# Third branch of a hybrid mixer on one Trainium2 core: keys normed and the decay's input prepared between the projected tiles

## The chip, the cores and the metric

The kernel runs on one core of a Trainium2 chip. The metric is the device time of one execution in microseconds (us), as a median of several runs; lower is better. All data is f32. Five engines work side by side, each in the order of its own program, and wait for one another on semaphores: TensorE (PE; its weight loads are shown apart, as PEld), VectorE (DVE), ScalarE (ACT), GpSimd (POOL), and SyncE (SP), whose queue issues nearly all transfers.

## The reference, cut to what matters

Two layers (`DEPTH = 2`) over 256 context tokens and 256 image tokens with a model width of 1024. Each layer has a mixer of three branches (latent attention, an mLSTM, an RWKV-7 style recurrence), then 64 routed experts. The change is in the third branch, before its recurrence:

```python
r, k, v, wl, al, gl = jnp.split(centred_shift(z, mu), RW_SPLIT_IDX, axis=-1)
kk = (k * k_k).reshape(B, T, RW_HEADS, RW_N)
kk = kk / jnp.maximum(jnp.linalg.norm(kk, axis=-1, keepdims=True), 1e-12)
...
w = -jax.nn.softplus(-(w0[d] + jnp.tanh(wl_d) @ w2[d])) - 0.5
decay = jnp.exp(-jnp.exp(w))
a = jax.nn.sigmoid(a0[d] + al_d @ a2[d])
kd = k * (1 + (a - 1) * k_a)
...
g = jax.nn.sigmoid(gl) @ g2        # used once, at the branch's output
```

`z` is the layer's input times 1152 columns of `w_in`. Both directions d = 0 and 1 use the same `kk`; d = 1 runs over the tokens in reverse.

## The kernel before

Everything is held with features on the 128 partitions and the 512 tokens along the free axis. The third branch's projection makes nine tiles of 128 features, j = 0 to 8: r is in tiles 0 and 1, k in 2 and 3, v in 4 and 5, the decay's small input in 6, the rate's small input in 7, the output gate's input in 8. In the second layer tiles 0, 1 and 8 cover 256 tokens only. Each engine's part is a function, and each layer runs them in the order attention, mLSTM, third branch, merging of the branches, routing, experts.

- `rw_pe` (TensorE): tile j is 8 matmuls over the width (`project`, L292; a f32 matmul leaves two records) into bank j % 4. From j = 4 on it waits until ScalarE has copied out tile j - 4 (`zev`). After the nine tiles come, in this order: two 128x512 matmuls with a block-diagonal matrix of ones that sum the squared keys by head into banks 4 and 5 (L968; they wait for the square, `kc` 2), four small products of direction 0 with `w2` and `a2` (L986; they wait for `tl` 2) into banks 0 to 3, 32 small matmuls that turn v to rows (L992), the first of the late modulation rows (L309), then the turning of beta and kappa (L1003, waits for `prep`) and the score products (L1014).
- `rw_act` (ScalarE): copies tile j into one of two padded buffers `ZP` (L1125). After all nine: Tanh of tile 6 (L1127), Sigmoid of tile 8 (L1129), square of the keys (L1131), Ln and Exp that give the inverse norm (L1133, L1134), then for direction 0 the two sigmoids of each pair of heads (L1139, L1141), copies of the turned v (L1145), three exponentials for each pair (L1148 to L1150), and a copy of the modulation row (L315).
- `rw_dve` (VectorE): three operations shift tile j between neighbouring tokens and mix it into `Zs` (L1193 to L1195, counted in `sh`). After all nine: keys times `k_k` (L1198), the maximum with 1e-24 (L1205), keys times inverse norm (L1210). Then for each direction the prefix sum of the decay's logarithm (L1216) and its difference (L1218) for both pairs, and beta, kappa and AR (L1221 to L1234), the last of which releases L1003.

No planner orders the work: the order is the program text and the waits. SyncE's queue loads 2 MB chunks of weights into four ring slots. In this branch it loads the chunks for the late modulation rows into slots 0 and 1, each when the slot's earlier user has been read. The expert weights are issued only after the branches of that layer are merged.

Of the kernel before, what the change touches and what calls it, by code (L numbers as in the profile page):

```python
# [7 lines left out]
ALU = mybir.AluOpType  # L8
ACT = mybir.ActivationFunctionType
# [4 lines left out]
P = 128  # L14
# [143 lines left out]
def build(nc, xin, consts, smalls, wsm, wst, wexp, out):  # L158
    es = ExitStack()
    with es:  # L160
# [14 lines left out]
        WS = sb("small_weights", [P, WS_N])  # L175
# [7 lines left out]
        ps = [es.enter_context(nc.psum_tensor(f"bank{i}", [P, 512], F32)) for i in range(8)]  # L183
# [15 lines left out]
        def sm(name, j=0, n=1):  # L199
            return S_[:, SM[name] + j:SM[name] + j + n]  # L200
# [748 lines left out]
        def each_head():  # L949
            return (slice(0, 64), slice(64, 128))  # L950

        def opposite(h):

            return slice(64 - h.start, 128 - h.start)

        def rw_pe(pe, l):
            for j in range(9):
# [6 lines left out]
                if j == 1:  # L964
                    ml_turn_back(pe, l)
            pe.wait_ge(rw["kc"], l * RW["kc"] + 2)
            for i in range(2):
                last = nc.tensor.matmul(ps[4 + i][:, :], bd, YA[:, i, :], start=True, stop=True)  # L968
            last.then_inc(rw["kc"], 1)
            pe.wait_ge(rw["tl"], l * RW["tl"] + 2)  # L970
            for d in range(2):
# [10 lines left out]
                if d:  # L982
                    pe.wait_ge(rw["yc"], l * RW["yc"] + 2)
                for pr in PAIRS:
                    for i, (o, z, rows_of) in enumerate(((WS_W2, 6, hd_), (WS_A2, 7, opposite(hd_)))):
                        nc.tensor.matmul(ps[2 * pr + i][:, :], WS[rows_of, o + pr * P:o + (pr + 1) * P], Zs[rows_of, z, :], start=True, stop=True).then_inc(rw["lr"], 1)  # L986
                if d == 0:
# [117 lines left out]
            for pr in range(2):  # L1105
                last = nc.tensor.matmul(ps[2 + pr][:, c0:], bd, YA[:, pr, c0:], start=True, stop=True)
                last.then_inc(rw["ym"], 1)
            for pr in range(2):
                nc.tensor.matmul(ps[6 + pr][:, c0:], WS[:, WS_G2 + pr * P:WS_G2 + (pr + 1) * P], Zs[:, 8, c0:], start=True, stop=True).then_inc(rw["g"], 1)
# [6 lines left out]
        def rw_act(act, ch, l):  # L1116
            for j in range(9):
# [7 lines left out]
                nc.scalar.activation(dst, seg(ps[j % 4][:, :])[:, half:, :], ACT.Copy).then_inc(rw["zev"], 1)  # L1125
            act.wait_ge(rw["sh"], l * RW["sh"] + 9)
            nc.scalar.activation(Zs[:, 6, :], Zs[:, 6, :], ACT.Tanh).then_inc(rw["tl"], 1)  # L1127
            c0 = queries_from(l)
            nc.scalar.activation(Zs[:, 8, c0:], Zs[:, 8, c0:], ACT.Sigmoid).then_inc(rw["tl"], 1)  # L1129
            act.wait_ge(rw["kc"], l * RW["kc"] + 1)  # L1130
            nc.scalar.activation(YA[:, :, :], KK[:, :, :], ACT.Square).then_inc(rw["kc"], 1)  # L1131
            act.wait_ge(rw["kc"], l * RW["kc"] + 4)
            ch.link(nc.scalar.activation(KDS[:, :, :], KDS[:, :, :], ACT.Ln))  # L1133
            nc.scalar.activation(KDS[:, :, :], KDS[:, :, :], ACT.Exp, scale=-0.5).then_inc(rw["kc"], 1)  # L1134
            for d in range(2):
                mods = late_mod(l, d)
                for pr in PAIRS:
                    act.wait_ge(rw["lr"], l * RW["lr"] + 4 * d + 2 * pr + 1)
                    nc.scalar.activation(sgm[pr], ps[2 * pr][:, :], ACT.Sigmoid, bias=sm("w0", 2 * d + pr)).then_inc(rw["sg"], 1)  # L1139
                    act.wait_ge(rw["lr"], l * RW["lr"] + 4 * d + 2 * pr + 2)  # L1140
                    nc.scalar.activation(aa[pr], ps[2 * pr + 1][:, :], ACT.Sigmoid, bias=sm("a0", 2 * d + pr)).then_inc(rw["sg"], 1)  # L1141
                if d == 0:
                    for pr in PAIRS:
                        act.wait_ge(rw["tok"], l * RW["tok"] + pr + 1)
                        nc.scalar.activation(VT[pr][:, :, :], ps[4 + pr][:, :].rearrange("p (c f) -> p c f", c=NC), ACT.Copy).then_inc(rw["tokc"], 1)  # L1145
# [33 lines left out]
        def rw_dve(dve, ch, l):  # L1179
# [6 lines left out]
            for j in range(9):  # L1186
# [8 lines left out]
                nc.vector.scalar_tensor_tensor(seg(Zs[:, j, :])[:, half:, :], z[:, :, 1:257], omu[:, j:j + 1], t, ALU.mult, ALU.add).then_inc(rw["sh"], 1)  # L1195
            dve.wait_ge(rw["sh"], l * RW["sh"] + 9)
            for pr in range(2):
                last = nc.vector.tensor_scalar(KK[:, pr, :], Zs[:, 2 + pr, :], sm("k_k", pr), None, ALU.mult)  # L1198
                if pr == 0:
                    ch.add(last)  # L1200
            last.then_inc(rw["kc"], 1)

            dve.wait_ge(rw["kc"], l * RW["kc"] + 3)
            for pr in range(2):
                last = nc.vector.tensor_scalar(KDS[:, pr, :], ps[4 + pr][:, :], 1e-24, None, ALU.max)  # L1205
                if pr == 0:
                    ch.add(last)
            last.then_inc(rw["kc"], 1)
            dve.wait_ge(rw["kc"], l * RW["kc"] + 5)
            nc.vector.tensor_tensor(KK[:, :, :], KK[:, :, :], KDS[:, :, :], ALU.mult).then_inc(rw["kc"], 1)  # L1210
            dve.wait_ge(rw["kc"], l * RW["kc"] + 6)
# [1608 lines left out]
```

## Time and profile before

| | |
|---|---|
| median of 3 runs | 2665.92 us (2663.73 to 2675.43) |
| the profiled execution, its own time | 2670.35 us |
| its span in the trace | 2668.2 us, 41238 instructions |
| busy: PE, DVE, ACT, POOL | 2411.8, 785.9, 573.4, 145.9 us |
| mean granted TensorE clock | 0.949 of full |

The profile was taken of one execution, 4.43 us above the median. A row of the chain of work gives a start, a length and the instruction that the end of the kernel depended on at that time. A row of the timeline gives a start, a length, engine, line, operation, written and read tiles, and in brackets how long the engine had been idle and what ended that. The views by stretch give busy time and the granted clock, where 1.00 is the full 2.4 GHz and 0.50 is 1.2 GHz. "issue" is idle time for which the trace shows no wait.

### The profile page before, as it was taken

What the parts mean: (1) busy time and instruction counts of PE and PEld (TensorE: products, weight loads), DVE (VectorE), ACT (ScalarE), POOL (GpSimd) and SP (SyncE); (2) the same over time, 40 slices, a digit from 0 to 9 for tenths busy, and PEclk for the clock granted to TensorE, in tenths of its full rate; (3) what the DMA queues carried; (4) which work ended last, traced back from release to release, by engine and by line L of the source; (5) the groups of instructions that cost most, each with busy time, mean ns of one, the idle gap of its engine ahead of it and who ended that gap; (6) DMA issues with size and microseconds to landing.
All of it is one profiled execution on the core that took longest, in us unless ns stands there. A gap on an engine that the chain in (4) does not pass through costs nothing.

```text
span 2668.2 us, 41238 instructions
## 1 busy us (share of the span) xinstructions
PE 2411.8 (90%) x17286; PEld 1365.4 (51%) x17286; DVE 785.9 (29%) x1929; ACT 573.4 (21%) x1134; POOL 145.9 (5%) x154
## 2 busy tenths in 40 slices
PE   7999978999998898999998789978999798977997
PEld 3466467744445443333333556747788644433444
DVE  1354355311113531111111525455411521111112
ACT  3445123120003011111111144333220211100111
POOL 0000000000000011111111000000000011100100
PEclk9999989999997899999999999989999799988999
DMA  7201032521101699999999631113241599999993
GB/s 318 79 2 39 32 128 99 185 98 64 63 0 63 250 424 423 409 407 424 404 407 393 257 144 72 64 37 124 101 186 63 201 374 422 420 408 417 413 423 153
DMA packets 67640, 599.72 MB, mean 225 GB/s; under 512 B 13182, under 2 KB 13310, under 8 KB 25600
## 3 DMA queue, kind: packets, MB, share of 16 engines
q1 hardware_dynamic: 50032, 555.09, 51.3%
q0 software_dynamic: 17424, 41.99, 4.1%
q8 instruction: 137, 2.24, 0.3%
q14 instruction: 47, 0.39, 0.0%
HBM read 588.63 MB, written 26.75 MB: 231 GB/s over the span
## 4 chain that ended last, share of the span: by engine, by line
PE 79%; DMA 9%; DVE 6%; issue 4%; ACT 2%; SPq 0%; ACTq 0%; DVEq 0%
PE bank L1855 10%; PE bank L1330 9%; PE bank L292 6%; PE bank L2281 5%; PE bank L1870 5%; DMA ring<-in_wexp 3%; PE bank L1345 3%; PE bank L2295 3%; PE bank L1335 3%; DMA arena<-in_wexp 3%; PE bank L384 3%; PE bank L2301 2%; PE bank L1026 2%; PE bank L1041 2%; PE bank L309 1%
## 5 line engine op out<-in xcount | busy, mean ns | idle before, releaser
L1855 PE MATMUL bank<-ring,arena 128*32 128x512 f32 (+2 forms) x1248 | 299.1, 610 | 16.7 <-issue 14.7
L1330 PE MATMUL bank<-normed,ring 128*128 128x512 f32 (+1 forms) x768 | 255.5, 486 | 0.0
L2281 PE MATMUL bank<-ring,arena 128*32 128x512 f32 (+2 forms) x832 | 192.8, 624 | 16.5 <-issue 15.0
L1330 PEld LDWEIGHTS bank<-normed,ring 128*128 128x128 f32 x768 | 145.9, 190 | 101.8 <-issue 91.8
L1855 PEld LDWEIGHTS bank<-ring,arena 128*32 128x32 f32 (+2 forms) x1248 | 95.2, 131 | 152.6 <-issue 150.4
L292 PE MATMUL bank<-normed,ring 128*128 128x512 f32 (+1 forms) x416 | 160.2, 544 | 0.0
L1855 PE MATMUL bank<-branches,arena 128*32 128x512 f32 (+2 forms) x400 | 137.3, 610 | 8.1 <-issue 8.1
L292 PEld LDWEIGHTS bank<-normed,ring 128*128 128x128 f32 x416 | 78.4, 190 | 77.8 <-issue 75.3
L1870 PE MATMUL bank<-arena 128*32 128x512 f32 (+2 forms) x384 | 112.7, 596 | 3.9 <-DMA arena<-in_wexp 2.0
L2045 DVE TENSOR_TENSOR arena<-bank,arena 128x256 f32<-128x256 f32 x43 | 18.2, 424 | 327.5 <-ACT arena L1964 327.5
L2281 PEld LDWEIGHTS bank<-ring,arena 128*32 128x32 f32 (+2 forms) x832 | 56.1, 123 | 102.1 <-issue 102.0
L1784 POOL DMA_INDIRECT arena<-hidden_rows,block_slots x42 | 42.7, 1016 | 1186.2 <-DVE block_slots L1601 900.5
L2295 PE MATMUL bank<-arena 128*32 128x512 f32 (+1 forms) x400 | 87.2, 654 | 21.6 <-issue 21.0
L1870 PE MATMUL bank<-ring,arena 128*32 128x512 f32 (+2 forms) x440 | 102.0, 596 | 4.0 <-issue 2.0
L2281 PE MATMUL bank<-normed,arena 128*32 128x512 f32 (+1 forms) x256 | 90.4, 628 | 15.9 <-issue 15.1
L2301 PE MATMUL bank<-arena 128*128 128x256 f32 x432 | 97.7, 380 | 1.1 <-DVE arena L2471 1.1
L2465 DVE TENSOR_TENSOR arena<-bank,arena 128x256 f32<-128x256 f32 x27 | 11.5, 424 | 294.6 <-ACT arena L2397 294.6
L2281 PE MATMUL bank<-branches,arena 128*32 128x512 f32 (+1 forms) x208 | 96.7, 620 | 0.0
L1335 PE MATMUL bank<-branches,ring 128*128 128x512 f32 (+1 forms) x256 | 90.4, 486 | 0.0
L2301 PEld LDWEIGHTS bank<-arena 128*128 128x128 f32 x432 | 80.0, 190 | 12.6 <-issue 2.8
L384 PE MATMUL bank<-normed,ring 128*128 128x512 f32 (+1 forms) x192 | 77.9, 567 | 8.7 <-DMA ring<-in_wst 8.7
L1345 PE MATMUL bank<-arena,ring 128*128 128x512 f32 (+1 forms) x256 | 83.1, 486 | 2.6 <-DVE arena L1374 2.6
(485 smaller groups left out, 3779.2 us busy)
## 6 DMA issues: line engine op xcount, KB each, us to landing
ring<-in_wexp SPq DMA_DIRECT2D x87, 2048.0 KB, 19.1
ring<-in_wst SPq DMA_DIRECT2D x54, 2048.0 KB, 8.4
arena<-in_wexp SPq DMA_DIRECT2D x70, 1024.0 KB, 20.5
branches<-in_wexp SPq DMA_DIRECT2D x31, 2048.0 KB, 18.2
ring<-in_wexp SPq DMA_DIRECT2D x60, 1024.0 KB, 19.7
normed<-in_wexp SPq DMA_DIRECT2D x12, 2048.0 KB, 19.4
arena<-expert_rows SPq DMA_DIRECT2D x6, 2048.0 KB, 10.9
branches<-expert_rows SPq DMA_DIRECT2D x2, 2048.0 KB, 14.4
```

The source lines that it names most:

```text
L292: last = nc.tensor.matmul(bank[:, c0:], weights[:, k, j0:j0 + n], H[:, k, c0:], start=(k == 0), stop=(k == KD - 1))
L384: last = nc.tensor.matmul(ps[j][:, c0:], w[:, k, (j % 4) * P:(j % 4 + 1) * P], H[:, k, c0:], start=(k == 0), stop=(k == KD - 1))
L1026: last = nc.tensor.matmul(ps[4 + pr][h, cc], NL[pr][h, cc], XT[pr][h, cc] if v else ident[h, h], start=True, stop=True)
L1041: last = nc.tensor.matmul(ps[pr][h, cc], ZT[pr][h, cc], X[pr][h, cc], start=True, stop=True)
L1330: last = nc.tensor.matmul(ps[2 * (n % 4)][:, c0:], wg[:, k, i * P:(i + 1) * P], H[:, k, c0:], start=(k == 0), stop=(k == KD - 1))
L1335: last = nc.tensor.matmul(ps[2 * (n % 4) + 1][:, c0:], wb[:, k, :], BR[:, k, c0:], start=(k == b0), stop=(k == b1 - 1))
L1345: last = nc.tensor.matmul(ps[m % 4][:, c0:], w[:, k, (m % 4) * P:(m % 4 + 1) * P], YM[:, k, c0:], start=(k == 0), stop=(k == KD - 1))
L1855: last = nc.tensor.matmul(ps[2 + s][r0:r1, :], XT_[:, s, k * P + r0:k * P + r1], wt[:, k, :], start=(k == 0), stop=(k == KD - 1))
L1870: last = nc.tensor.matmul(ps[5 + h][r0:r1, :], HDT[:, s, k * P + r0:k * P + r1], wt[:, k, h * 512:(h + 1) * 512], start=(k == 0), stop=(k ...
L2281: last = nc.tensor.matmul(ps[5][r0:r1, :], XT_[:, s, k * P + r0:k * P + r1], w[:, k, :], start=(k == 0), stop=(k == KD - 1))
L2295: last = nc.tensor.matmul(ps[6 + h][r0:r1, :], HDT[:, s, k * P + r0:k * P + r1], w[:, k, h * 512:(h + 1) * 512], start=(k == 0), stop=(k = ...
L2301: last = nc.tensor.matmul(acc(m), YB[s][:, m * P:(m + 1) * P], OH[s], start=False, stop=False)
```

## The change

On all three engines the keys' norm is moved into the loop over the tiles. VectorE multiplies the keys by `k_k` after tile 3, ScalarE squares them after tile 4, TensorE sums them after tile 5, VectorE takes the maximum after tile 5, ScalarE does Ln and Exp after tile 6, VectorE scales the keys after tile 7. Tanh of tile 6 follows ScalarE's copy of tile 7. Direction 0's four small products stand right behind tile 8 and use the banks 2 and 3 for the first pair and 0 and 1 for the second (`small_bank`); the first pair waits for eight tiles copied out and no longer for the output gate's Sigmoid, which ScalarE does after direction 0's four sigmoids. Direction 1 keeps its banks.

```diff
+        def small_bank(d, pr):
+
+            return (2 * pr + 2 * (1 - d)) % 4
...
                 if j == 1:
                     ml_turn_back(pe, l)
-            pe.wait_ge(rw["kc"], l * RW["kc"] + 2)
-            for i in range(2):
-                last = nc.tensor.matmul(ps[4 + i][:, :], bd, YA[:, i, :], start=True, stop=True)
-            last.then_inc(rw["kc"], 1)
-            pe.wait_ge(rw["tl"], l * RW["tl"] + 2)
+                if j == 5:
+                    pe.wait_ge(rw["kc"], l * RW["kc"] + 2)
+                    for i in range(2):
+                        last = nc.tensor.matmul(ps[4 + i][:, :], bd, YA[:, i, :], start=True, stop=True)
+                    last.then_inc(rw["kc"], 1)
+            pe.wait_ge(rw["tl"], l * RW["tl"] + 1)
+            pe.wait_ge(rw["sh"], l * RW["sh"] + 8)
...
                 for pr in PAIRS:
+                    if d == 0:
+                        pe.wait_ge(rw["zev"], l * RW["zev"] + 8 + pr)
                     for i, (o, z, rows_of) in enumerate(((WS_W2, 6, hd_), (WS_A2, 7, opposite(hd_)))):
-                        nc.tensor.matmul(ps[2 * pr + i][:, :], WS[rows_of, o + pr * P:o + (pr + 1) * P], Zs[rows_of, z, :], start=True, stop=True).then_inc(rw["lr"], 1)
+                        nc.tensor.matmul(ps[small_bank(d, pr) + i][:, :], WS[rows_of, o + pr * P:o + (pr + 1) * P], Zs[rows_of, z, :], start=True, stop=True).then_inc(rw["lr"], 1)
...
+            pe.wait_ge(rw["tl"], l * RW["tl"] + 2)
             for pr in range(2):
                 nc.tensor.matmul(ps[6 + pr][:, c0:], WS[:, WS_G2 + pr * P:WS_G2 + (pr + 1) * P], Zs[:, 8, c0:], start=True, stop=True).then_inc(rw["g"], 1)
...
-            act.wait_ge(rw["sh"], l * RW["sh"] + 9)
-            nc.scalar.activation(Zs[:, 6, :], Zs[:, 6, :], ACT.Tanh).then_inc(rw["tl"], 1)
+                if j == 4:
+                    act.wait_ge(rw["kc"], l * RW["kc"] + 1)
+                    nc.scalar.activation(YA[:, :, :], KK[:, :, :], ACT.Square).then_inc(rw["kc"], 1)
+                if j == 6:
+                    act.wait_ge(rw["kc"], l * RW["kc"] + 4)
+                    ch.link(nc.scalar.activation(KDS[:, :, :], KDS[:, :, :], ACT.Ln))
+                    nc.scalar.activation(KDS[:, :, :], KDS[:, :, :], ACT.Exp, scale=-0.5).then_inc(rw["kc"], 1)
+                if j == 7:
+                    act.wait_ge(rw["sh"], l * RW["sh"] + 7)
+                    nc.scalar.activation(Zs[:, 6, :], Zs[:, 6, :], ACT.Tanh).then_inc(rw["tl"], 1)
             c0 = queries_from(l)
-            nc.scalar.activation(Zs[:, 8, c0:], Zs[:, 8, c0:], ACT.Sigmoid).then_inc(rw["tl"], 1)
-            act.wait_ge(rw["kc"], l * RW["kc"] + 1)
-            nc.scalar.activation(YA[:, :, :], KK[:, :, :], ACT.Square).then_inc(rw["kc"], 1)
-            act.wait_ge(rw["kc"], l * RW["kc"] + 4)
-            ch.link(nc.scalar.activation(KDS[:, :, :], KDS[:, :, :], ACT.Ln))
-            nc.scalar.activation(KDS[:, :, :], KDS[:, :, :], ACT.Exp, scale=-0.5).then_inc(rw["kc"], 1)
...
                 if d == 0:
+                    act.wait_ge(rw["sh"], l * RW["sh"] + 9)
+                    nc.scalar.activation(Zs[:, 8, c0:], Zs[:, 8, c0:], ACT.Sigmoid).then_inc(rw["tl"], 1)
                     for pr in PAIRS:
                         act.wait_ge(rw["tok"], l * RW["tok"] + pr + 1)
...
-            dve.wait_ge(rw["sh"], l * RW["sh"] + 9)
-            for pr in range(2):
-                last = nc.vector.tensor_scalar(KK[:, pr, :], Zs[:, 2 + pr, :], sm("k_k", pr), None, ALU.mult)
...
+                if j == 3:
+                    dve.wait_ge(rw["sh"], l * RW["sh"] + 4)
+                    for pr in range(2):
+                        last = nc.vector.tensor_scalar(KK[:, pr, :], Zs[:, 2 + pr, :], sm("k_k", pr), None, ALU.mult)
...
+                if j == 5:
+                    dve.wait_ge(rw["kc"], l * RW["kc"] + 3)
+                    for pr in range(2):
+                        last = nc.vector.tensor_scalar(KDS[:, pr, :], ps[4 + pr][:, :], 1e-24, None, ALU.max)
...
+                if j == 7:
+                    dve.wait_ge(rw["kc"], l * RW["kc"] + 5)
+                    nc.vector.tensor_tensor(KK[:, :, :], KK[:, :, :], KDS[:, :, :], ALU.mult).then_inc(rw["kc"], 1)
```

## Rows read from the trace of the kernel before

**Rows 1.** The page: rate of transfers in 40 slices; the whole chain by engine.

```profile
GB/s 318 79 2 39 32 128 99 185 98 64 63 0 63 250 424 423 409 407 424 404 407 393 257 144 72 64 37 124 101 186 63 201 374 422 420 408 417 413 423 153
...
PE 79%; DMA 9%; DVE 6%; issue 4%; ACT 2%; SPq 0%; ACTq 0%; DVEq 0%
```

**Rows 2.** The chain of work, first layer, around the change: start, us, what.

```profile
271.39 48.08 PE bank L292 x112
...
325.73 3.39 PE bank L968 x4
...
335.99 1.24 DVE arena L1216
...
342.09 0.69 DVE arena L1231
...
344.64 3.68 PE bank L1003 x64
```

**Rows 3.** The chain of work, second layer, the same place.

```profile
1734.88 18.49 PE bank L292 x51
...
1769.04 1.24 DVE arena L1216
...
1777.42 3.68 PE bank L1003 x64
...
1784.57 1.86 PE bank L1003 x64
```

**Rows 4.** The timeline, first layer, 319 to 342 us.

```profile
319.49 0.60 ACT L1125 ACTIVATE arena<-bank 128x512 f32<-128x512 f32 x1 [6.27 <-PE bank L292]
...
321.37 0.75 DVE L1195 SCALAR_TENSOR_TENSOR arena<-arena 128x512 f32<-128x512 f32 x1
...
322.16 0.88 DVE L1198 TENSOR_SCALAR arena<-arena,smalls 128x512 f32<-128x512 f32 x2
...
324.10 0.63 ACT L1129 ACTIVATE arena<-arena 128x512 f32<-128x512 f32 x1
324.63 1.04 ACT L1131 ACTIVATE arena<-arena 128x1024 f32<-128x1024 f32 x1
...
329.03 1.99 PE L986 MATMUL bank<-arena,small_weights 64*128 64x512 f32 x8
329.14 1.29 DVE L1205 TENSOR_SCALAR arena<-bank 128x512 f32<-128x512 f32 x2 [6.09 <-PE bank L968]
...
331.53 1.28 ACT L1134 ACT_TABLE_LOAD   x1
332.83 1.06 ACT L1134 ACTIVATE arena<-arena 128x1024 f32<-128x1024 f32 x1
332.96 1.90 PE L309 MATMUL bank<-ring,condv 128*2 128x512 f32 x16
...
333.92 1.23 DVE L1210 TENSOR_TENSOR arena<-arena 128x1024 f32<-128x1024 f32 x1 [3.49 <-ACT arena L1134]
...
335.20 0.69 ACT L1139 ACTIVATE arena<-bank,smalls 128x512 f32<-128x512 f32 x1
...
339.90 0.63 ACT L1148 ACTIVATE arena<-arena 128x512 f32<-128x512 f32 x1
...
340.96 0.61 ACT L1150 ACTIVATE arena<-arena 128x512 f32<-128x512 f32 x1
```

**Rows 5.** The timeline, second layer, 1753 to 1759 us.

```profile
1753.40 0.38 ACT L1125 ACTIVATE arena<-bank 128x256 f32<-128x256 f32 x1 [2.86 <-PE bank L292]
...
1754.66 0.48 DVE L1195 SCALAR_TENSOR_TENSOR arena<-arena 128x256 f32<-128x256 f32 x1
...
1758.54 3.61 PE L968 MATMUL bank<-arena,consts 128*128 128x512 f32 x4 [5.18 <-ACT arena L1131]
```

**Rows 6.** Stretch of two us: busy us of PE, PEld, DVE, ACT, POOL; granted clock; DMA share; GB/s.

```profile
1772.00:1774.00 2.00, 0.00 (x0) 0.00 (x0) 1.93 (x5) 1.99 (x3) 0.00 (x0) 0.60 1.07 451
```

**Rows 7.** The timeline of PE, first layer, 383 us.

```profile
383.63 1.12 PE L1026 MATMUL bank<-ring 64*64 64x64 f32 x16 [2.25 <-issue]
```

More of the change, by code:

```diff
@@ L1138, in rw_act @@
                     act.wait_ge(rw["lr"], l * RW["lr"] + 4 * d + 2 * pr + 1)
-                    nc.scalar.activation(sgm[pr], ps[2 * pr][:, :], ACT.Sigmoid, bias=sm("w0", 2 * d + pr)).then_inc(rw["sg"], 1)
+                    nc.scalar.activation(sgm[pr], ps[small_bank(d, pr)][:, :], ACT.Sigmoid, bias=sm("w0", 2 * d + pr)).then_inc(rw["sg"], 1)
                     act.wait_ge(rw["lr"], l * RW["lr"] + 4 * d + 2 * pr + 2)
-                    nc.scalar.activation(aa[pr], ps[2 * pr + 1][:, :], ACT.Sigmoid, bias=sm("a0", 2 * d + pr)).then_inc(rw["sg"], 1)
+                    nc.scalar.activation(aa[pr], ps[small_bank(d, pr) + 1][:, :], ACT.Sigmoid, bias=sm("a0", 2 * d + pr)).then_inc(rw["sg"], 1)
                 if d == 0:
+                    act.wait_ge(rw["sh"], l * RW["sh"] + 9)
+                    nc.scalar.activation(Zs[:, 8, c0:], Zs[:, 8, c0:], ACT.Sigmoid).then_inc(rw["tl"], 1)
                     for pr in PAIRS:
@@ L1195, in rw_dve @@
                 nc.vector.scalar_tensor_tensor(seg(Zs[:, j, :])[:, half:, :], z[:, :, 1:257], omu[:, j:j + 1], t, ALU.mult, ALU.add).then_inc(rw["sh"], 1)
-            dve.wait_ge(rw["sh"], l * RW["sh"] + 9)
-            for pr in range(2):
-                last = nc.vector.tensor_scalar(KK[:, pr, :], Zs[:, 2 + pr, :], sm("k_k", pr), None, ALU.mult)
[L1199 to L1210, printed above, removed]
+                if j == 3:
+                    dve.wait_ge(rw["sh"], l * RW["sh"] + 4)
+                    for pr in range(2):
+                        last = nc.vector.tensor_scalar(KK[:, pr, :], Zs[:, 2 + pr, :], sm("k_k", pr), None, ALU.mult)
+                        if pr == 0:
+                            ch.add(last)
+                    last.then_inc(rw["kc"], 1)
+                if j == 5:
+                    dve.wait_ge(rw["kc"], l * RW["kc"] + 3)
+                    for pr in range(2):
+                        last = nc.vector.tensor_scalar(KDS[:, pr, :], ps[4 + pr][:, :], 1e-24, None, ALU.max)
+                        if pr == 0:
+                            ch.add(last)
+                    last.then_inc(rw["kc"], 1)
+                if j == 7:
+                    dve.wait_ge(rw["kc"], l * RW["kc"] + 5)
+                    nc.vector.tensor_tensor(KK[:, :, :], KK[:, :, :], KDS[:, :, :], ALU.mult).then_inc(rw["kc"], 1)
             dve.wait_ge(rw["kc"], l * RW["kc"] + 6)
```

## The prediction, made before the changed kernel ran

> **What bounds the kernel now.** I read the page first. The chain that ends last is TensorE for 79% of the span, and transfers run above 390 GB/s only in two stretches of slices, the two expert phases [rows 1]. The change lies outside them, in the third branch of each layer, so the question is what ends last there. For that I read the chain around the branch in both layers. In the first layer TensorE's projection ends at 271.39 + 48.08 = 319.47 us, and the next thing that TensorE does on the chain with real length, L1003, starts at 344.64: 25.2 us. Between them lie VectorE and ScalarE one at a time and the 3.39 us of L968 [rows 2]. In the second layer the same stretch is 1734.88 + 18.49 = 1753.37 to 1777.42, 24.1 us [rows 3]. So here the dependent sequence sets the time. During the projection the reverse holds: ScalarE had been idle for 6.27 us before it could copy tile 8 [rows 4].
>
> Then I read the timeline of the stretch for the durations. I call E the end of tile 8's matmuls. The event by which I measure is the start of the first prefix sum (L1216): 335.99, or E + 16.52, in the first layer [rows 2], and 1769.04, or E + 15.67, in the second [rows 3]. Everything after it, 8.65 us (344.64 - 335.99) and 8.38 us (1777.42 - 1769.04) to L1003, has the same operations before and after the change.
>
> **What leaves the path and what it costs inside the projection.** One record of a projection matmul takes 48.08/112 = 0.429 us [rows 2], so a full tile of 16 takes 6.87 us and a half tile in the second layer 3.43 us.
>
> - TensorE, L968: four records go between tile 5 and tile 6. They are on the path there, since TensorE sets the pace. At the rate of its neighbours they cost 4 x 0.429 = 1.72 us. In the gap they took 3.39 us in the first layer [rows 2] and 3.61 us in the second [rows 5]. The ends of this unknown are 1.72 and 3.39 for a layer; I take 1.72, because the rows beside it run at that rate, and TensorE has no pause before it.
> - Its wait for the square: the keys are shifted 2.65 us after tile 3 ends (321.37 + 0.75 - 319.47), L1198 adds 0.88, and the square (1.04) comes after tile 4 is copied (0.60) [rows 4]. It is ready 1.7 us after tile 4 and 5.2 us before tile 5 ends. Cost nothing; should it be late, tiles 6 to 8 wait behind it.
> - VectorE, the maximum: L968 ends 1.7 us after tile 5, VectorE is done with the tile's shift at 2.65 us, and 1.29 us more ends at 3.9 of 8.6 us until tile 6 ends [rows 4]. Hidden. What is queued behind it is the shift of tile 6.
> - ScalarE, Ln and Exp with two table loads: 0.60 for the copy of tile 6, then 1.28 + 1.06 + 1.28 + 1.06 = 4.68, in all 5.3 us, against 6.87 us until tile 7 can be copied [rows 4]. Hidden with 1.6 us to spare in both layers, as tile 7 is a full tile in both. Behind it wait the copy of tile 7, its shift and Tanh. TensorE would not notice before tile 8 had been done, because its banks are four tiles deep.
> - Tanh is as long as the Sigmoid beside it, 0.63 us [rows 4], and ends 1.3 us after tile 7; the shift of tile 7 ends at 2.65. Both lie before E, even where tile 8 is half as long. VectorE's product by the inverse norm, 1.23 us [rows 4], ends 3.9 us after tile 7, which is E + 0.5 in the second layer; tile 8 is copied at E + 0.4 (0.38 us [rows 5]), so the last shift is held 0.1 us, with slack behind it.
>
> **The path after the change, first layer.** Direction 0's first pair of small products can start at E, in banks that were copied before. Two 64-row products stand beside each other; all four took 1.99 us, so the first pair is through by E + 1.0 [rows 4]. ScalarE copies tile 8 until 320.09, loads the Sigmoid table in 1.28 us, starts the first sigmoid at 321.41 and ends it 0.69 us later [rows 4]: 322.10. VectorE's last shift ends at 322.12 [rows 4]. The prefix sum began 0.10 us after the sigmoid's end (335.20 + 0.69 against 335.99 [rows 2, 4]), hence at 322.20, E + 2.73. Gain: 335.99 - 322.20 = 13.79, less 1.72: 12.07 us.
>
> **Second layer.** The half tile is copied until 1753.78, the load ends at 1755.08, the sigmoid starts at 1755.10 and ends at 1755.79, and the prefix sum starts at 1755.89, E + 2.52. The last shift ended at 1754.66 + 0.48 = 1755.14 [rows 5] and is no limit. Gain: 1769.04 - 1755.89 = 13.15, less 1.72: 11.43 us.
>
> **What could be late next.** The gate's Sigmoid now stands before the exponentials that AR needs. From the first sigmoid to the first exponential it was 339.90 - 335.20 = 4.70 us, table load included; the moved Sigmoid adds 0.53 (0.63 less the overlap of neighbouring ones, 0.10), and the third exponential ends 1.67 us on (340.96 + 0.61 - 339.90) [rows 4]. So it is ready at E + 1.94 + 5.23 + 1.67 = E + 8.84. AR started 342.09 - 335.99 = 6.10 us after the prefix sum [rows 2], so now at E + 8.83. The two meet; cost 0.0. In the second layer the Sigmoid covers half the columns, and ScalarE is ahead. The copies of v come some 2.5 us before the first exponential, at E + 4.7, and TensorE has turned v by E + 3.9 (332.96 - 329.03 [rows 4]). No DMA is added. The one chunk that the queue issues after the first modulation rows starts earlier by as much as they do, and no read of it is pulled nearer.
>
> Sum: 12.07 + 11.43 = 23.5 us. Of the profiled execution's own 2670.35 us that leaves 2646.9; it stood 4.43 us above the median, so I set the median at 2665.92 - 23.5 = **2642.4 us**. The expert weights are issued only after the branches have been merged, so these phases start earlier and I cost them at nothing.
>
> **TensorE's clock.** After the change TensorE works from E to E + 5.83 (329.03 to 334.86 [rows 4]) and then waits for L1003 until E + 11.38 in the first layer and E + 10.90 in the second: idle for 5.5 and 5.1 us. Before, in the second layer, it had been idle from about 1767.9 (1758.54 + 3.61 + 5.83 [rows 4, 5]) and the granted clock fell to 1.2 GHz at 1772.4, where the mean of 0.60 puts it [rows 6], 4.5 us in; and after an idle 5.18 us its four records of L968 took 0.90 us each, twice the 0.43 [rows 5]. I expect the fall to happen again, so L1003 starts at the low level as before (3.68 us against 1.86 for the second pair at 2.4 GHz [rows 3]) and nothing is gained. If it does not fall, 1.82 us a layer are.
>
> **A rule against this sum.** The row of the table load shows 1.28 us, and the activation behind it starts 0.02 us after its end (331.53 + 1.28 = 332.81, start 332.83 [rows 4]). That is what the sum uses. The Trainium skill (page "ScalarE: Activation LUTs", section "What ACT_TABLE_LOAD costs") gives the same load and a drain of some 1.38 us on top, 2.66 us for each switch. By that an estimate gives 1.4 us for each load that is now on the path, two a layer, and 5.5 us less gain, 2648. The trace shows no such time here.
>
> **The rivals.**
>
> - Forecast: 2642.4 us, chance 0.60. Its own scatter is some 4 us either way.
> - The clock stays at 2.4 GHz over the shortened pause: 3.6 us more gain, 2638.8 us. For it, 5.5 and 5.1 us are near the 4.5 us after which it fell; against it, the fall after 5.18 us idle [rows 5]. 0.14.
> - A table load costs twice its row where ScalarE is now alone on the path. The first sigmoid is 1.3 us later, and the exponentials 2.6 us: 5.2 us less gain over two layers, 2647.6 us. Against it stands the 0.02 us behind the load. 0.04.
> - TensorE stalls at L1003 or the score products. It now runs them while the 2 MB chunk of the modulation rows is under way; at 383.63 it had stood still 2.25 us with no wait in the trace [rows 7]. With the low clock that can follow (1.82 [rows 3]) that is 4.1 us a layer, 8.1 in both, 2650.5 us. For it, that stall is real; against it, the trace shows one such in many overlaps. 0.12.
> - The expert phases scatter. The three runs lie 11.7 us apart; all of that against me gives 2654.1 us, no change that can be told. 0.07.
> - The other side: the expert phases' transfers run slower in the new program. They fill 15 slices of 66.7 us at 374 to 424 GB/s [rows 1], about 1000 us. To be slower by 0.5% they must lose 23.5 + 13.3 = 36.8 us, so it decides from 3.7% less rate on, and at 4% gives 2682 us. The slices differ by more than that among themselves, but nothing in the change touches them. 0.03.
>
> **How the numbers follow.** Within 0.5% (13.3 us, about what a measurement of this kernel can tell from no change) means above 2652.6 us. The forecast, the clock and the table case lie on the faster side, the stall case for the most part: 0.86. No measurable change is the scatter case and the rest of the stall case: 0.11. Slower: 0.03. The range runs from 2633 us (the clock case with its scatter) to 2652 us (the stall case, and L968 at its upper bound of 3.39 in both layers, which would be 2645.7); beyond it lie the last two rivals and a part of the stall case, some 0.15.
>
> **What the changed profile would show.** L968 as four records of about 0.43 us inside the projection with no pause before or behind. No ScalarE row later than its tile's copy by the table loads: tile 7 copied right at its matmuls' end. L986 at E, the first sigmoid at E + 1.9, the prefix sum at E + 2.7 and E + 2.5, L1003 at E + 11.4 and E + 10.9, against 25.2 and 24.1 before. I am wrong if the table load starts only once the small products are through, if ScalarE's exponentials hold AR back, if a PE pause appears between tiles 5 and 6, or if the branch gets its 23 us and the span does not.

## The result, and the profile after

The changed kernel took 2642.82 us (median of 4 runs, 2636.76 to 2646.11), the kernel before 2666.78 us beside it. The ratio is 0.9895, 95% interval 0.9878 to 0.9913. A second set of runs gave 0.9911 (0.9897 to 0.9926). The prediction was 2642.4 us, in a range of 2633 to 2652.

The profiled execution took 2640.6 us of span against 2668.2. Its page shows the same 17286 matmul records, ScalarE two instructions fewer, and a slightly higher share of TensorE on the chain:

```profile
PE 2402.9 (91%) x17286; PEld 1365.7 (52%) x17286; DVE 785.4 (30%) x1929; ACT 570.4 (22%) x1132; POOL 146.3 (6%) x154
...
PE 82%; DMA 7%; DVE 5%; issue 3%; ACT 2%; another core or an unknown queue 0%; SPq 0%; ACTq 0%; DVEq 0%
```

The two instructions that are gone are table loads, one a layer: the old order went from Tanh to a Sigmoid and back to Ln. In this kernel L973 is the sum by head (before: L968), L994 the small products (L986), L1140 and L1141 are Ln and Exp, L1150 the decay's sigmoid (L1139), L1155 the gate's Sigmoid (L1129), L1231 the prefix sum (L1216), L1246 the first AR product (L1231), L1011 the turning of beta (L1003), L1034 the first product of each level of the inverse (L1026).

The chain of work in the first layer, which answers to [rows 2]:

```profile
299.67 1.72 PE bank L973 x4
301.39 20.60 PE bank L292 x48
321.99 1.97 PE bank L994 x8
323.96 0.67 ACT arena L1150
...
326.36 0.52 ACT arena L1155
...
327.87 1.28 ACT L1161
...
329.16 0.63 ACT arena L1161
...
330.93 0.69 DVE arena L1246
...
333.49 3.48 PE bank L1011 x64
```

The sums cost 1.72 us in the projection, to the hundredth what was taken for them. The projection ends at 321.99, and L1011 follows at 333.49, 11.5 us later and not 25.2. Between them the chain now goes through ScalarE in an unbroken row: four sigmoids, the gate's Sigmoid, two copies, a table load, the exponentials. VectorE's prefix sum is no longer on it.

In the second layer, which answers to [rows 3], the prefix sum is on it, 2.5 us behind the tile's end at 1722.16 + 17.20 = 1739.36, and L1011 comes 10.9 us behind it:

```profile
1722.16 17.20 PE bank L292 x48
1739.38 0.38 ACT arena L1134
1739.79 1.28 ACT L1150
1741.08 0.70 ACT arena L1150
1741.87 1.24 DVE arena L1231
...
1750.26 3.37 PE bank L1011 x64
...
1756.31 1.86 PE bank L1011 x64
```

The timeline of the first layer shows what ScalarE does between the tiles:

```profile
308.30 0.60 ACT L1134 ACTIVATE arena<-bank 128x512 f32<-128x512 f32 x1 [7.99 <-PE bank L292]
308.91 1.28 ACT L1140 ACT_TABLE_LOAD   x1
310.20 1.06 ACT L1140 ACTIVATE arena<-arena 128x1024 f32<-128x1024 f32 x1
311.28 1.28 ACT L1141 ACT_TABLE_LOAD   x1
312.57 1.06 ACT L1141 ACTIVATE arena<-arena 128x1024 f32<-128x1024 f32 x1
315.16 0.60 ACT L1134 ACTIVATE arena<-bank 128x512 f32<-128x512 f32 x1 [1.53 <-PE bank L292]
...
324.73 1.23 DVE L1231 TENSOR_TENSOR_SCAN arena<-consts,arena 128x512 f32<-128x512 f32 x1
...
333.49 3.48 PE L1011 MATMUL bank<-consts,arena 64*64 64x64 f32 x64 [5.74 <-DVE arena L1249]
```

After Exp it was idle 1.53 us before tile 7 came: the slack of 1.6. The prefix sum starts at 324.73, E + 2.74. TensorE was idle 5.74 us before L1011 and ran it at 1.2 GHz. The stretches of two us (columns as in [rows 6]) show the granted clock fall and come back:

```profile
328.00:330.00 2.00, 0.00 (x0) 0.00 (x0) 1.97 (x4) 1.99 (x3) 0.00 (x0) 0.94 0.80 147
330.00:332.00 2.00, 0.00 (x0) 0.00 (x0) 1.83 (x5) 2.00 (x5) 0.00 (x0) 0.50 0.90 385
...
336.00:338.00 2.00, 2.00 (x44) 2.00 (x44) 2.00 (x4) 0.98 (x2) 0.00 (x0) 0.85 0.00 0
```

The mean of 0.94 puts the fall at 329.8 us, 2 us after TensorE's last matmul (327.75). In the second layer, where the stretch 1748 to 1750 has 0.93, it fell 4.6 us after the last matmul (1745.11).

Stage by stage, from two profiles of each kernel, in us. E is again the end of tile 8's matmuls, taken 0.02 before ScalarE's copy of it starts; the recurrence runs from the turning of beta to the first sum at the branch's end (L1104, now L1112).

| stretch | before, two profiles | after, two profiles |
|---|---|---|
| E to turning of beta, layer 1 | 25.2, 25.6 | 11.5, 11.5 |
| both recurrences, layer 1 | 185.7, 180.7 | 178.6, 178.4 |
| from there to E of layer 2 | 1223.1, 1225.7 | 1227.4, 1224.7 |
| E to turning of beta, layer 2 | 24.0, 24.1 | 10.9, 10.9 |
| both recurrences, layer 2 | 157.0, 160.7 | 157.2, 157.3 |

The changed stretch is the same to 0.4 us in each pair: 49.2 less 22.4 less 2 x 1.72 for the sums is 23.4 us. The rest of the first pair's 27.6 us of span is in stretches that also differ by up to 5 us between two executions of one kernel. Two profiles of each kernel can't tell whether a few us of it belong to the change all the same.

### The profile page after: what moved, and what is told of

Same layout as the page of the kernel before. It is cut to its first block, busy times and chain, and to the rows that moved or that the text cites. A ratio compares the mean times of both kernels' runs of the same rounds, so it can differ in the third digit from the quotient of the medians.

```text
span 2640.6 us, 41238 instructions
## 1 busy us (share of the span) xinstructions
PE 2402.9 (91%) x17286; PEld 1365.7 (52%) x17286; DVE 785.4 (30%) x1929; ACT 570.4 (22%) x1132; POOL 146.3 (6%) x154
## 4 chain that ended last, share of the span: by engine, by line
PE 82%; DMA 7%; DVE 5%; issue 3%; ACT 2%; another core or an unknown queue 0%; SPq 0%; ACTq 0%; DVEq 0%
PE bank L1870 10%; PE bank L1345 9%; PE bank L2296 7%; PE bank L292 6%; PE bank L1885 5%; PE bank L2310 3%; PE bank L1360 3%; PE bank L1350 3%; PE bank L2316 3%; PE bank L384 3%; DMA ring<-in_wexp 2%; DMA arena<-in_wexp 2%; PE bank L1034 2%; PE bank L1049 2%; PE bank L309 1%
## 5 line engine op out<-in xcount | busy, mean ns | idle before, releaser
L1345 PE MATMUL bank<-normed,ring 128*128 128x512 f32 (+1 forms) x768 | 255.5, 486 | 0.0
L2296 PE MATMUL bank<-ring,arena 128*32 128x512 f32 (+2 forms) x832 | 193.4, 621 | 18.1 <-issue 16.6
L292 PE MATMUL bank<-normed,ring 128*128 128x512 f32 (+1 forms) x416 | 160.5, 544 | 0.0
L2060 DVE TENSOR_TENSOR arena<-bank,arena 128x256 f32<-128x256 f32 x43 | 18.3, 425 | 324.0 <-ACT arena L1979 324.0
L2296 PE MATMUL bank<-normed,arena 128*32 128x512 f32 (+1 forms) x256 | 92.9, 644 | 21.0 <-issue 18.1
L2480 DVE TENSOR_TENSOR arena<-bank,arena 128x256 f32<-128x256 f32 x27 | 11.5, 425 | 301.2 <-ACT arena L2412 301.2
L2310 PE MATMUL bank<-arena 128*32 128x512 f32 (+1 forms) x400 | 82.1, 630 | 17.4 <-issue 16.8
L1372 ACT ACTIVATE arena<-bank 128x512 f32<-128x512 f32 (+1 forms) x48 | 23.4, 490 | 286.2 <-PE bank L1345 286.2
## 6 DMA issues: line engine op xcount, KB each, us to landing
branches<-expert_rows SPq DMA_DIRECT2D x2, 2048.0 KB, 14.4
```

What stands on the lines that cost most here:

```text
L292: last = nc.tensor.matmul(bank[:, c0:], weights[:, k, j0:j0 + n], H[:, k, c0:], start=(k == 0), stop=(k == KD - 1))
L1345: last = nc.tensor.matmul(ps[2 * (n % 4)][:, c0:], wg[:, k, i * P:(i + 1) * P], H[:, k, c0:], start=(k == 0), stop=(k == KD - 1))
L2296: last = nc.tensor.matmul(ps[5][r0:r1, :], XT_[:, s, k * P + r0:k * P + r1], w[:, k, :], start=(k == 0), stop=(k == KD - 1))
L2310: last = nc.tensor.matmul(ps[6 + h][r0:r1, :], HDT[:, s, k * P + r0:k * P + r1], w[:, k, h * 512:(h + 1) * 512], start=(k == 0), stop=(k = ...
```

## The experiments

Each timed experiment ran beside the kernel before. Its ratio is to that kernel, with the 95% interval. The branch's own numbers are from the profile.

**The changed kernel once more.**

> The changed kernel once more, for a tighter ratio and a second profile. Theory (the dependent sequence behind the last tile sets the time, 23.5 us shorter in all): ratio 0.991, and in the new profile the prefix sum again 2.7 and 2.5 us behind the end of tile 8. Rival (a good part of the gain came from other places: the first profile shows some 7 us won inside the first layer's recurrence and some 3 us given back later, which may be one execution's luck): then the second profile's stages differ from the first by several us outside the changed stretch, while the changed stretch is the same to 0.3 us.

Ratio 0.9911 (0.9897 to 0.9926). The prefix sum came 2.7 and 2.5 us behind E. The stretches outside it differ by 3 us between the two profiles of this kernel (table above). The theory holds; the 7 us that the first profile won in the first recurrence are taken up below.

**The norm alone.**

```diff
-            pe.wait_ge(rw["tl"], l * RW["tl"] + 1)
-            pe.wait_ge(rw["sh"], l * RW["sh"] + 8)
+            pe.wait_ge(rw["tl"], l * RW["tl"] + 2)
+            pe.wait_ge(rw["sh"], l * RW["sh"] + 9)
...
-                if j == 7:
-                    act.wait_ge(rw["sh"], l * RW["sh"] + 7)
-                    nc.scalar.activation(Zs[:, 6, :], Zs[:, 6, :], ACT.Tanh).then_inc(rw["tl"], 1)
+            act.wait_ge(rw["sh"], l * RW["sh"] + 9)
+            nc.scalar.activation(Zs[:, 6, :], Zs[:, 6, :], ACT.Tanh).then_inc(rw["tl"], 1)
             c0 = queries_from(l)
+            nc.scalar.activation(Zs[:, 8, c0:], Zs[:, 8, c0:], ACT.Sigmoid).then_inc(rw["tl"], 1)
```

(The small products are in their old banks, and their wait for `zev` is gone.)

> One part alone: the keys' norm stays in the projection, but Tanh and the gate's Sigmoid follow tile 8 as before and the small products wait for both, in the old banks. Theory: behind the end of tile 8 come copy 0.6, shift 2.0, Tanh 0.63, table load 1.28, Sigmoid 0.63, small products about 1.0, sigmoid 0.69: prefix sum at 7.0 us in the first layer and 5.9 in the second, so 7.8 and 8.1 us are gained, 15.9 in all, ratio to before 0.994. Rival (the norm's sequence had been the whole of the wait): all of the 23.5 us, 0.991.

Ratio 0.9947 (0.9929 to 0.9964), 14.2 us. The prefix sum came at E + 8.2 and E + 7.1, so the profile gives 6.6 and 6.8 us, 13.4 in all. It is 1.2 us a layer later than expected, and the timeline of the first layer shows why (E is 321.62):

```profile
326.93 3.78 PE L992 MATMUL bank<-arena,small_weights 64*128 64x512 f32 x8 [5.32 <-ACT arena L1143]
329.03 0.69 ACT L1148 ACTIVATE arena<-bank,smalls 128x512 f32<-128x512 f32 x1 [2.16 <-PE bank L992]
```

The small products wait 5.32 us for the Sigmoid, and TensorE then does them at 1.2 GHz: 3.78 us against 1.99 in the changed kernel, where they stand right behind the tile. The turning of v behind them is slow too, 2.83 us against 2.08, and in the first layer that delays ScalarE's copies and exponentials until they hold AR:

```profile
337.20 0.69 DVE L1242 TENSOR_TENSOR arena<-arena 128x512 f32<-128x512 f32 x1 [1.30 <-ACT arena L1159]
```

So turning of beta is at E + 18.1 and E + 15.6. Measured there, the part is worth 5.3 and 6.7 us, 12.0 in all.

**The small products alone.** The whole norm goes back behind tile 8 (with its waits), the rest stays as changed:

```diff
-                if j == 4:
-                    act.wait_ge(rw["kc"], l * RW["kc"] + 1)
-                    nc.scalar.activation(YA[:, :, :], KK[:, :, :], ACT.Square).then_inc(rw["kc"], 1)
...
             c0 = queries_from(l)
+            act.wait_ge(rw["kc"], l * RW["kc"] + 1)
+            nc.scalar.activation(YA[:, :, :], KK[:, :, :], ACT.Square).then_inc(rw["kc"], 1)
+            act.wait_ge(rw["kc"], l * RW["kc"] + 4)
+            ch.link(nc.scalar.activation(KDS[:, :, :], KDS[:, :, :], ACT.Ln))
+            nc.scalar.activation(KDS[:, :, :], KDS[:, :, :], ACT.Exp, scale=-0.5).then_inc(rw["kc"], 1)
```

> The other part alone: Tanh early, small products right behind tile 8 in the new banks, gate's Sigmoid late, but the whole norm of the keys behind tile 8 as before (the square's sums behind the small products, ScalarE's square, Ln and Exp ahead of the four sigmoids). Theory: prefix sum 13.2 us behind tile 8 in the first layer and 12.3 in the second; gain 3.3 and 3.4 us, 6.7 in all, ratio to before 0.9975; with norm_only's 15.9 this is 22.6 of the 23.5. Rival (the small products' wait was the main part): above 12 us, 0.9955 or less.

Ratio 0.9987 (0.9976 to 0.9997), 3.5 us. The prefix sum came at E + 14.4 and E + 12.7, so 2.1 and 3.0 us, 5.1 in all. In the first layer TensorE had paused before the sums, which took 2.77 us and not 1.72 as its clock fell under them. The two parts give 18.5 us by the prefix sum, the change 23.5. By the turning of beta they give 12.0 + 5.0 = 17.0 us, the change 23.4. Each part alone leaves TensorE a pause in front of a product that is on the path (5.32 us with the norm alone, 2.81 us before these sums).

**The norm one tile later.**

```diff
-                if j == 5:
+                if j == 6:
                     pe.wait_ge(rw["kc"], l * RW["kc"] + 2)
...
-                if j == 6:
+                if j == 7:
                     act.wait_ge(rw["kc"], l * RW["kc"] + 4)
```

(On VectorE the maximum moves to j == 6 and the product to j == 8.)

> The changed kernel with sums, maximum, Ln, Exp and the last product each one tile later (sums after tile 6, Ln and Exp after tile 7 and ahead of Tanh, product after the shift of tile 8). Theory (ScalarE has 1.6 us to spare in a full tile's time, and none in the half tile of the second layer): first layer prefix sum 1.2 us later, by the product alone; second layer 3.2 us later, since Tanh and the copy of tile 8 wait for Ln and Exp; 4.4 us slower than the changed kernel, ratio to before 0.9927. Rival (place in the projection does not matter as long as it is hidden behind matmuls): the same as the changed kernel within 1 us.

Ratio 0.9936 (0.9922 to 0.9950), 6.7 us behind the changed kernel of the same set. The prefix sum is at E + 3.8 and E + 5.2, so 1.1 and 2.7 us later where 1.2 and 3.2 were expected. Turning of beta is at E + 12.5 and E + 14.1, 1.0 and 3.2 us later, 4.2 in all. The profile has the rest in the recurrence (184.1 us in the first layer, below). In the second layer the copy of the half tile waits behind Exp and Tanh, and the small products with it:

```profile
1742.46 1.06 ACT L1141 ACTIVATE arena<-arena 128x1024 f32<-128x1024 f32 x1
1743.43 0.61 ACT L1143 ACTIVATE arena<-arena 128x512 f32<-128x512 f32 x1
1743.95 0.36 ACT L1134 ACTIVATE arena<-bank 128x256 f32<-128x256 f32 x1
1744.09 2.63 PE L994 MATMUL bank<-arena,small_weights 64*128 64x512 f32 x8 [2.49 <-ACT arena L1143]
```

So the place in the projection does matter, by ScalarE's time between two tiles.

**The sums made twice.**

```diff
-                    for i in range(2):
+                    for i in (0, 1, 0, 1):
```

> The changed kernel with the two sums of the squared keys made twice, all inside the projection. Theory (TensorE sets the pace there and these cost what their neighbours do): 1.72 us more in each layer, 3.4 us slower than the changed kernel, ratio to before 0.9925. Rival (the sums are hidden or cost the 3.4 us of the low clock): 0 or 6.8 us.

Ratio 0.9935 (0.9911 to 0.9959), 17.4 us, 6.4 less than the changed kernel's 23.8. The chain gives 3.43 us for the eight records, so 1.72 a layer more as expected:

```profile
299.74 3.43 PE bank L973 x8
```

The remaining 3 us are not at the sums: its recurrence of the first layer took 186.8 us. By the ratio alone neither 3.4 nor 6.8 us would be refused. The chain decides.

**The small products in their old banks.**

```diff
-            return (2 * pr + 2 * (1 - d)) % 4
+            return 2 * pr
...
-                        pe.wait_ge(rw["zev"], l * RW["zev"] + 8 + pr)
+                        pe.wait_ge(rw["zev"], l * RW["zev"] + 9)
```

> The changed kernel with the small products of direction 0 in their old banks, so that the first pair waits for tile 8's copy, 0.6 us behind its matmuls in the first layer and 0.4 in the second. Theory (ScalarE's table load ends 1.9 us behind tile 8, the products are through by 1.6): the first sigmoid and the prefix sum start where they did, no difference. Rival (the products gate the sigmoid): 0.6 and 0.4 us later, 1.0 us in all.

Ratio 0.9913 (0.9897 to 0.9929), no difference. TensorE did wait 0.78 us for the copy, and the prefix sum came at 324.45, E + 2.72, all the same:

```profile
321.75 0.60 ACT L1134 ACTIVATE arena<-bank 128x512 f32<-128x512 f32 x1 [5.75 <-PE bank L292]
322.37 1.28 ACT L1150 ACT_TABLE_LOAD   x1
...
322.49 1.99 PE L994 MATMUL bank<-arena,small_weights 64*128 64x512 f32 x8 [0.78 <-ACT arena L1134]
...
323.66 0.69 ACT L1150 ACTIVATE arena<-bank,smalls 128x512 f32<-128x512 f32 x1
```

The table load covers it. The exchange of banks is worth nothing here.

**Keeping TensorE's clock.** Matmuls that nobody reads fill its pause, first in direction 0, then in both:

```diff
                 rows(0)
+                for _ in range(5 + 2 * d):
+                    nc.tensor.matmul(ps[7][:, :], bd, YA[:, 0, :], start=True, stop=True)
```

(`fill_first` has `5 if d == 0 else 0`.)

> The changed kernel with five 128x512 matmuls more (ones by head times the squared keys, into bank 7, read by nobody) behind direction 0's first modulation rows, 4.3 us of TensorE's pause of 5.7 and 5.1 us. Theory of the clock (TensorE's granted clock falls in this pause and costs the first half of the turning of beta and kappa): it stays at 1.00, L1011's first group takes 1.9 us in place of 3.5 and 3.4, 3.1 us faster in all than the changed kernel. Rival (the clock fell for another reason, or the faster TensorE only waits for VectorE): same as the changed kernel.

> As fill_first, and seven such matmuls in direction 1, whose pause is 7.0 and 6.7 us in the changed kernel. Theory: L1011's first groups take 1.9 us in place of 3.7 there too; 7 us faster than the changed kernel in all, ratio to before 0.9880. Rival: no more than fill_first.

Ratios 0.9921 (0.9904 to 0.9939) and 0.9909 (0.9892 to 0.9926): no faster than the changed kernel (0.9911 in another set). At its place the filling did what the clock theory says: the granted clock is 1.00 in every stretch of two us from 324 to 340. The timeline of PE in `fill_first` (E is 320.93):

```profile
332.41 2.08 PE L1013 MATMUL bank<-consts,arena 64*64 64x64 f32 x64 [1.25 <-DVE arena L1251]
...
337.82 2.03 PE L1013 MATMUL bank<-consts,ring 64*64 64x64 f32 x64
```

The second turning starts at E + 16.9, in the changed kernel at 340.30, E + 18.3: 1.4 us won, and 2.08 us where there were 3.48. But the recurrences took 178.7 and 165.1 us, where the changed kernel had 178.6 and 157.2. It was given back further on, at a place that the theory had not looked at.

**Where it is given back.** All profiles have idle time of TensorE for which they show no wait, within the levels of the inverse. In the changed kernel, first layer, with the queue's issue of a 2 MB chunk ahead of it:

```profile
364.40 0.33 SPq L2587 DMA_DIRECT2D ring<-in_wst  x1
```

```profile
369.21 0.41 PE L1034 MATMUL bank<-ring 64*64 64x64 f32 x6
371.88 0.97 PE L1034 MATMUL bank<-ring 64*64 64x64 f32 x26 [2.26 <-issue]
372.78 1.05 PE L322 MATMUL bank<-consts,arena 98*128 98x2 f32 x8
373.77 3.27 PE L309 MATMUL bank<-ring,condv 128*2 128x512 f32 x16
```

TensorE stops in the middle of a group, 5.2 us after the issue, and afterwards the rows product takes 3.27 us and not 1.90, as the clock has fallen. All such stops above 0.8 us and the length of the recurrences:

| kernel | stops, us, layer 1; recurrences | stops, us, layer 2; recurrences |
|---|---|---|
| before (two profiles) | 5.2; 185.7 and 3.0; 180.7 | none; 157.0 and 2.6; 160.7 |
| changed (two profiles) | 3.4; 178.6 and 3.2; 178.4 | none; 157.2 and none; 157.3 |
| norm_only | 3.0; 177.0 | none; 157.1 |
| small_only | 4.9; 178.3 | 2.4; 162.1 |
| norm_late | 5.4; 184.1 | none; 157.0 |
| sum_twice | 5.4; 186.8 | 2.5; 161.4 |
| fill_first, fill_both | 4.6; 178.7 and 3.0; 178.7 | 2.8; 165.1 and 2.9; 160.9 |
| old_banks | 2.8; 177.1 | none; 156.8 |

So 7 to 10 us between variants lie in stretches that the edits don't touch. The length of the stops doesn't order the rows by itself: `small_only` has 4.9 us of them and 178.3 us, `sum_twice` 5.4 us and 186.8. The rest is TensorE's busy time in the same 3816 records, 156.6 against 164.2 us, at a mean granted clock of 0.96 against 0.92.

Four single profiles were to tell the cause. The kernel before once more:

> The kernel before once more, for a second profile. In nine other profiles TensorE stood still for 0.9 to 2.4 us without a wait in the trace, 4.4 to 6.7 us after a 2 MB chunk was issued wherever the two issue times can be told apart. Theory (the place is set by the program, where the supply of TensorE's instructions meets a big transfer): the same three stalls in the first layer's recurrence as in the first profile of this kernel, and the time from the turning of beta to the end of the recurrence is again 186 us, where the changed kernel has 178. Rival (chance of an execution): other places, and 178 to 187.

The stop at 383.5 is in the same place, in the middle of the same group (after 7 of 32 records) and again 5.2 us after the issue, now 1.93 us long:

```profile
383.07 0.41 PE L1026 MATMUL bank<-ring 64*64 64x64 f32 x7
385.41 1.36 PE L1026 MATMUL bank<-ring 64*64 64x64 f32 x25 [1.93 <-issue]
```

A second stop is in its old place too, after two records of L322. The first line is of the first profile, the second of the new one:

```profile
495.75 0.83 PE L322 MATMUL bank<-consts,arena 98*128 98x2 f32 x6 [0.92 <-issue]
...
490.71 0.83 PE L322 MATMUL bank<-consts,arena 98*128 98x2 f32 x6 [1.02 <-issue]
```

The stop of 2.04 us at 479 in the first profile is missing, and the second layer, which had none, has 2.6 us. The recurrences of the first layer took 180.7 us and not 186. The theory held for two of three places: the place is largely set by the program, and whether TensorE stops there is partly chance of the execution.

Then the late modulation chunks cut to a sixteenth, in three kernels:

```diff
-                    sp.dma_start(in_slot(slot(m, j))[:, 0:CH_COLS[j]], wst[m, j, :, 0:CH_COLS[j]]).then_inc(chunk_in[slot(m, j)], 16)
+                    cols_in = 256 if j < N_MOD_CH and not (m == 0 and j < MOD_FIRST) else CH_COLS[j]
+                    sp.dma_start(in_slot(slot(m, j))[:, 0:cols_in], wst[m, j, :, 0:cols_in]).then_inc(chunk_in[slot(m, j)], 16)
```

> The kernel before, with only 256 of 4096 columns loaded of each late modulation chunk (the modulation values are then wrong, and what follows in the expert phases is not compared, only the branch). Theory (big transfers cause the stalls): no idle time of TensorE without a wait above 0.8 us in the recurrences, and from the turning of beta to the end of the recurrence under 177 us in the first layer, from 186. Rival: stalls stay.

> The changed kernel with the same short loads (256 of 4096 columns, the modulation values wrong). Theory: from the end of tile 8 to the turning of beta as in the changed kernel, 11.5 and 10.9 us; from there to the end of the recurrence the same as the kernel before with short loads to 1 us, since the change does nothing there. Rival (the change itself shortens the recurrence by starting its transfers earlier): several us less than that kernel.

> fill_both with the same short loads (256 of 4096 columns, the modulation values wrong). Theory (the filling did keep the clock and won 1.4 to 1.8 us at each of four places, which its stalls ate): from the turning of beta to the end of the recurrence 3.2 us less than the changed kernel with short loads in each layer. Rival (TensorE at the higher clock only waits for VectorE): no less.

The stops are gone: no such idle time above 0.6 us in any of the three, in either layer. The first layer's recurrences took 170.7, 171.2 and 169.8 us, the second layer's 156.1, 155.9 and 153.5. So the big transfers bring the stops about, and without them the kernel before and the changed one are equal there to 0.5 us: the change does nothing to the recurrence. Of the 15.0 us that the short loads save the kernel before in the first layer (185.7 - 170.7), 5.4 are idle time of this kind. Most of the rest is TensorE's busy time, 154.2 us against 164.6. Whole executions of these three took 2880 to 2916 us. The stretch between the branches alone took 1387 to 1393 us, presumably for the wrong modulation values, so only the branch is compared.

The filling is worth 1.4 and 2.4 us, less than the 3.2 a layer that were expected. `fill_loads` has short stops that `after_loads` hasn't, 0.8 us in the first layer and 1.0 in the second. They can be some of the missing 1.8 and 0.8 us. How much stays open.

The traces also show what ends a stop. A queue that the profile calls "instruction" moves 16 KB packets, 30 in the first layer's recurrences, for some 7630 records of matmuls and weight loads. In the changed kernel the stop from 369.62 to 371.88 us has one of them at its start, at 369.45, 0.93 us long (stretch 369.4 to 370.4 us):

```profile
q8 instruction: 1, 0.02, 5.8%
```

TensorE goes on 1.50 us after that packet's end. All 35 stops above 0.8 us in the eleven profiles end 1.20 to 1.56 us after such a packet's end, and so do the short ones of `fill_loads` (1.38 to 1.50). The packet of 369.45 is the sixth in the recurrences, and it starts when 790 of their matmul records have started. With short loads the sixth starts when 681 have. In the kernel before it is 791 against 705. So what TensorE waits for in a stop is its next instructions, and their packet comes late while a 2 MB transfer is under way. No run changed the supply of instructions by itself, so this rests on the times alone.

## Why the prediction was right

- **The bound.** Right. The dependent sequence behind tile 8 set the time in both layers; in `norm_only`, `small_only` and `norm_late` the time moves with what they move in it, though the ratios (14.2, 3.5 and 6.7 us) and the profiles (12.0, 5.0 and 4.2 us) agree to 2.5 us only.
- **L968 inside the projection, 1.72 us a layer.** Right, by the chain (1.72), and doubling it doubles the row (3.43).
- **The path after the change.** E + 2.73 and E + 2.52 were forecast for the prefix sum; 2.74 and 2.51 were measured. Turning of beta was forecast at E + 11.38 and E + 10.90; it came at 11.50 and 10.90.
- **Hidden work.** Right: 1.53 us of idle time in ScalarE where 1.6 were expected, and norm_late shows what lies behind that slack.
- **"The two meet; cost 0.0"** for the gate's Sigmoid. Off by 0.1 us: AR began 6.20 us behind the prefix sum and not 6.10 (330.93 - 324.73), held by the third exponential, and the chain now goes through ScalarE. That was one of the signs of being wrong, and it came true by this 0.1 us in the first layer only.
- **The clock falls again.** Right that it falls: 0.50 from 330 us on, L1011 at 3.48 and 3.37 us. The 4.5 us after which it had fallen was no guide: it fell 2 us into the pause in the first layer and 4.6 us in the second, so the shortened pause was not near to keeping it there. That L1011 would get 1.82 us from keeping it was near: 1.4 were measured by filling.
- **A table load.** The next activation again starts 0.01 us behind its end (308.91 + 1.28, then 310.20). Neither the rival of the doubled load nor the drain that the Trainium skill (page "ScalarE: Activation LUTs", section "What ACT_TABLE_LOAD costs") adds is seen in this trace; the change would have been some 5 us smaller by either.
- **The stall of TensorE.** I placed it at L1011 or the score products, with the chunk that now overlaps them. There was none there. There are stalls of the kind of [rows 7] in every profile with full loads, in the levels of the inverse, and with the slower clock behind them they are worth more than I gave them: 7 to 10 us between programs and up to 5 between executions. That the sum met the median to 0.4 us is therefore partly luck; its 23.5 us agree with the 23.4 of the changed stretch, and the two measured ratios give 28 and 24 us.
- **The expert phases.** 1223 to 1227 us between the branches, with no shift that two profiles can tell.

## What to carry to other kernels

When engines hand one small tensor back and forth behind a long TensorE phase, look inside that phase for the idle time of the others: here each tile left ScalarE 6.27 us, and 4.7 us of Ln, Exp and their loads went in for 1.72 us of TensorE. Check the shortest interval, not the usual one, since a half tile holds back the next step. And where an edit should bring 3 us, read its place in the profile: the ratio of whole runs carries stalls elsewhere that the edit only moves about.

## What the runs showed of the hardware that was not expected

- TensorE stands still for 0.9 to 2.6 us in the middle of a group of small matmuls, 4.4 to 6.8 us after a 2 MB transfer is issued, in all eleven profiles with full loads, and in none of the three with loads a sixteenth as long. It goes on 1.20 to 1.56 us after a 16 KB packet of the instruction queue has landed, in all 35 stops. The rows product behind one took 3.27 us and not 1.90.
- Behind a pause of 5.3 us a product on the path took twice as long (3.78 against 1.99 us, granted clock 0.50), so a dependent step costs more alone than right behind other matmuls. The clock fell 2.0 to 4.6 us into the pauses read here.
- Filling a pause with matmuls that nobody reads did keep 2.4 GHz and won 1.4 us at its place, and won nothing in the whole that the intervals could tell.
